# MLP up projections by seven half-token products for two tiles, with one low part of the weights on VectorE

## The chip, the cores and the metric

The program runs on one core of one Trainium2 chip. The metric is the device time of one launch in microseconds, as the median of several runs. TensorE (PE) multiplies and writes PSUM; VectorE (DVE), ScalarE (ACT) and GpSimd (POOL) do elementwise work; SyncE (SP) issues the loads of weights.

## The reference

Three transformer blocks over 512 tokens of width 1024. Two of them end in an MLP with a squared ReLU, and the change touches these alone:

```python
def squared_relu_mlp(h, w1, w2):
    return jnp.square(jax.nn.relu(h @ w1)) @ w2
...
        h = rms_norm(x, g[2])
        x = x + rms_norm(squared_relu_mlp(h, mlp_w1[i], mlp_w2[i]), g[3])
```

`w1` is 1024 x 4096 and `w2` 4096 x 1024, in float32. Before and after the MLPs stand attention, a convolution block and a gated feed-forward layer, which stay as they are.

## The kernel before

Activations lie transposed: 128 features on the partitions, 512 tokens along the free axis, 8 such tiles for a width of 1024. Every float32 operand is split into a high part (rounded to the matmul's format) and a low part (the difference), and every product is made of three matmuls: high x high, high x low, low x high (`products`, L1834 to L1836).

**Weights** come in blocks of 8 slots of 128x128, one block for one tile of outputs. There is a ring of 4 blocks in each of `raw`, `wh` and `wl`. For block n, SP loads `raw` when the low part of block n - 4 has been made (`load_range`), ScalarE copies it into `wh` when TensorE is through with block n - 4 (`hi`), and GpSimd subtracts the two into `wl` (`lo_range`, L548). TensorE waits for `w_lo`.

**The MLP** of a layer goes in 2 chunks of 16 hidden tiles. The up phase of a chunk has 16 tiles of 8 x 3 matmuls with 512 columns; the down phase has 8 output tiles with 16 x 3 matmuls each, from two blocks of weights. The up tiles rotate through four PSUM banks. Their input is the residual, not yet divided by its root mean square, so VectorE multiplies a tile by the square of that factor, `r2` (L1211), then makes max(z, 0) times that product with one `scalar_tensor_tensor` into a PSUM bank, `squared(j)` (L1219). ScalarE copies it into `HH` as the high part (L999), and VectorE subtracts the two into `HL` (L1211). The input of VectorE's instructions here is thus in PSUM on one side at least. In a down phase VectorE copies each finished bank to `M`, or adds it in the second chunk.

Every engine works through its own queue in the order of the program, and waits stand in it as instructions: what stands behind a wait waits too. Nothing else sets the order. `tmp` and `sqb` are buffers of 2 x 512 elements in SBUF, `RB`, `HB` and `META_BANK` are PSUM banks. The norms at both ends of an MLP use `HB`, `META_BANK`, `sqb` and `tmp` too.

## Time and profile before

| what | before |
|---|---|
| median of 3 runs | 1766.42 us (1766.36 to 1768.12) |
| profiled execution: its span, from the first to the last instruction | 1764.2 us |
| what lies between that span and the median of the runs | 2.2 us |
| instructions | 22985 |

The profile is of one execution. It gives that execution's time as its span; the times of the runs also hold what lies before the first and after the last instruction. In a row of the timeline the first number is the start in us from the start of the span, the second the duration; "x2" joins two instructions. A matmul's recorded duration is longer than its share of the array, since matmuls overlap: read the distance of their starts.

### The profile page before, as it was taken

To read this page: it belongs to the slowest core of one execution; us is meant where nothing else is said; L and a number is where in the kernel's file an instruction comes from. 1 tells how busy PE (TensorE), PEld (TensorE's weight loads), DVE (VectorE), ACT (ScalarE), POOL (GpSimd) and SP (SyncE) were. 2 spreads that over 40 slices of the span, in tenths; PEclk is the share of its full clock that TensorE was granted. 3 is DMA by queue.
4 is the path that set the end of the run, shared out by engine and by line. 5 is a ranking of instruction groups with operands and counts; after the bars stand their busy time and mean duration, and the time that the engine had idled before them with its cause. 6 is when DMAs were issued, how large, how long until landed. Compare 5 with 4: busy or idle time off the path is not lost.

```text
span 1764.2 us, 22985 instructions
## 1 busy us (share of the span) xinstructions
PE 1737.4 (98%) x8243; PEld 1445.3 (82%) x8243; DVE 785.8 (45%) x1225; ACT 662.9 (38%) x1039; POOL 876.9 (50%) x473
## 2 busy tenths in 40 slices
PE   8999999999999999999999999999999999999999
PEld 6887888888888877878888888889878888888887
DVE  6558654301331479956430133137856344444200
ACT  6338543312322456554321232135357332222221
POOL 3457545444444469755544444445445544444442
PEclk9999999999999999999999999999999999999999
DMA  5531123223333213123333332322210233332332
GB/s 190 133 98 59 37 72 107 95 95 96 96 96 99 80 48 108 60 84 95 103 99 96 96 95 95 95 84 72 87 49 14 95 95 96 97 101 98 96 107 71
DMA packets 46073, 158.45 MB, mean 90 GB/s; under 512 B 5744, under 2 KB 6000, under 8 KB 46000
## 3 DMA queue, kind: packets, MB, share of 16 engines
q1 hardware_dynamic: 46000, 157.45, 28.5%
q8 instruction: 49, 0.80, 0.2%
q14 instruction: 24, 0.20, 0.0%
HBM read 153.10 MB, written 2.10 MB: 88 GB/s over the span
## 4 chain that ended last, share of the span: by engine, by line
PE 90%; DVE 5%; ACT 2%; issue 1%; POOL 1%; DMA 0%; SPq 0%; DVEq 0%; POOLq 0%; ACTq 0%
PE PS L1834 26%; PE PS L1835 26%; PE PS L1836 26%; PE PS L1903 2%; DVE PS L1219 1%; PE PS L1939 1%; PE PS L1934 1%; PE PS L1935 1%; PE PS L2095 1%; PE PS L1844 1%; PE PS L1876 0%; PE PS L1976 0%; DVE PS L1211 0%; PE PS L2118 0%; PE PS L2119 0%
## 5 line engine op out<-in xcount | busy, mean ns | idle before, releaser
L548 POOL TENSOR_TENSOR wl<-raw,wh 128x1024 fp32r<-128x1024 f32 x216 | 523.0, 2422 | 623.2 <-ACT wh L742 198.3
L1835 PE MATMUL PS<-XLR,wh 128*128 128x512 f32 x1216 | 474.2, 390 | 0.0
L1834 PE MATMUL PS<-XHR,wh 128*128 128x512 f32 x888 | 348.8, 393 | 6.3 <-POOL wl L618 5.8
L1836 PE MATMUL PS<-XHR,wl 128*128 128x512 f32 x888 | 346.4, 390 | 0.0
L1834 PE MATMUL PS<-HH,wh 128*128 128x512 f32 x688 | 267.6, 389 | 0.0
L1835 PE MATMUL PS<-HL,wh 128*128 128x512 f32 x688 | 267.6, 389 | 0.0
L1836 PE MATMUL PS<-HH,wl 128*128 128x512 f32 x688 | 267.6, 389 | 0.0
L1835 PEld LDWEIGHTS PS<-XLR,wh 128*128 128x128 f32 x1216 | 229.1, 188 | 47.0
L728 ACT ACTIVATE wh<-raw 128x1024 fp32r<-128x1024 f32 x123 | 128.9, 1056 | 242.2 <-PE PS L1836 197.6
L1834 PEld LDWEIGHTS PS<-XHR,wh 128*128 128x128 f32 x888 | 167.4, 188 | 42.0 <-POOL wl L618 6.2
L1836 PEld LDWEIGHTS PS<-XHR,wl 128*128 128x128 f32 x888 | 167.4, 188 | 35.4
L1211 DVE TENSOR_TENSOR tmp<-PS,r2m 128x512 f32<-128x512 f32 x116 | 79.9, 691 | 253.2 <-PE PS L1836 235.7
L742 ACT ACTIVATE wh<-raw 128x1024 fp32r<-128x1024 f32 x68 | 72.1, 1061 | 284.3 <-PE PS L1836 284.3
L539 POOL TENSOR_TENSOR wl<-raw,wh 128x1024 fp32r<-128x1024 f32 x45 | 108.5, 2420 | 126.9 <-ACT wh L728 126.8
L1834 PEld LDWEIGHTS PS<-HH,wh 128*128 128x128 f32 x688 | 129.1, 188 | 26.9
L1836 PEld LDWEIGHTS PS<-HH,wl 128*128 128x128 f32 x688 | 129.1, 188 | 26.9
L1835 PEld LDWEIGHTS PS<-HL,wh 128*128 128x128 f32 x688 | 129.1, 188 | 26.7
L1834 PE MATMUL PS<-XF,wh 128*128 128x512 f32 x328 | 127.9, 390 | 0.1
L1836 PE MATMUL PS<-XF,wl 128*128 128x512 f32 x328 | 127.6, 389 | 0.0
L997 ACT ACTIVATE wh<-raw 128x1024 fp32r<-128x1024 f32 x56 | 59.4, 1060 | 164.2 <-PE PS L1836 164.2
L1190 ACT ACTIVATE wh<-raw 128x1024 fp32r<-128x1024 f32 x40 | 42.4, 1061 | 159.0 <-PE PS L1836 159.0
L578 POOL TENSOR_TENSOR prob<-prob,cols 128x512 f32<-128x512 f32 (+2 forms) x64 | 57.0, 893 | 40.8 <-DVE cols L1433 40.1
(344 smaller groups left out, 2561.6 us busy)
## 6 DMA issues: line engine op xcount, KB each, us to landing
raw<-weights SPq DMA_DIRECT2D x287, 512.0 KB, 3.5
X<-x_t SPq DMA_DIRECT2D x8, 256.0 KB, 6.7
out_t<-X SPq DMA_DIRECT2D x8, 256.0 KB, 4.7
KH<-rope_h SPq DMA_DIRECT2D x4, 128.0 KB, 4.7
KL<-rope_l SPq DMA_DIRECT2D x4, 128.0 KB, 5.5
QH<-XHR SPq DMA_DIRECT2D x16, 32.0 KB, 2.0
QL<-XLR SPq DMA_DIRECT2D x16, 32.0 KB, 2.0
pos_i<-positions SPq DMA_DIRECT2D x1, 256.0 KB, 8.5
```

What stands on the lines that cost most here:

```text
L539: pool.tensor_tensor(wl[:, n % RING], raw[:, n % RING], wh[:, n % RING].bitcast(F32), ALU.subtract).then_inc(w_lo, 1)
L548: pool.tensor_tensor(wl[:, j], raw[:, j], wh[:, j].bitcast(F32), ALU.subtract).then_inc(w_lo, 1)
L578: pool.tensor_tensor(p, p, cols[:, u % 4, 2:3].broadcast_to(p.shape), ALU.mult).then_inc(p_done, 1)
L728: sc.activation(wh[:, j], raw[:, j], ACT.Copy).then_inc(w_hi, 1)
L742: sc.activation(wh[:, j], raw[:, j], ACT.Copy).then_inc(w_hi, 1)
L997: sc.activation(wh[:, slot], raw[:, slot], ACT.Copy).then_inc(w_hi, 1)
L1190: sc.activation(wh[:, slot], raw[:, slot], ACT.Copy).then_inc(w_hi, 1)
L1211: return v.tensor_tensor(out, a, b, op)
L1834: pe.matmul(out, wa, xa, start=start, stop=False)
L1835: pe.matmul(out, wa, xb, start=False, stop=False)
L1836: return pe.matmul(out, wb, xa, start=False, stop=stop)
L1903: ins = pe.matmul(out[:, b], x, y[:, k, b * WIDE:(b + 1) * WIDE], start=first and k == 0, stop=last and k == KT - 1)
```

## The change

The hidden tiles of an MLP go in 4 chunks of 8, not 2 of 16. The up phase of the first chunk stays as it was, tile by tile. In the other three, two tiles make a group, which is computed as a product of matrices of two by two blocks: the two tiles, the two halves of the 1024 inputs (4 slots each), and the two halves of the tokens (256 columns each). Seven products of half blocks take the place of eight, in Winograd's form. Sums and differences of the four half blocks of weights of a group are made for each group; those of the four quarters of the activations once in a layer.

- **Activations.** During the down phase of the first chunk VectorE multiplies the residual by gain and factor into `CF` (`norm_halves`, eight instructions of 512), makes four combinations of 1024 (`combine_halves`), ScalarE makes seven high parts `CH`, and VectorE seven low parts `CL` in place of `CF`.
- **Weights of a group.** VectorE makes three sums of 512 into `sums` and in place in `raw` (`first_sums`) and a fourth later (`last_sum`), ScalarE five high parts (a11, s12 of double size, mid of double size, s4, a22). GpSimd makes the low parts of a11, s12, mid and s4; VectorE that of a22, the fourth raw half block (`low_a22`). The weights of the next group are made during the products of a group; those of the first group of a chunk during the down phase ahead of it.
- **Outputs of a group.** The products gather in two PSUM banks, `alpha` and `beta`, and a third, `gamma`. ScalarE copies what stands in them at four moments to the quarters of `tmp` (`z_part`), VectorE adds the other bank to three of them and squares each hidden tile in place, ScalarE copies it to `MH`, VectorE subtracts into `ML`. One buffer of 512 in `tmp` serves for each of the two tiles of a group.
- **Around it.** The down phases have 8 slots a tile and wait for each hidden tile by itself; VectorE copies to `M` in the first chunk and adds in three. A block "even" with one slot is put before the second MLP, so that its blocks start at an even slot of the ring. The loops of the MLP are unrolled. `low_taps` moves from the end of the first chunk's up phase to the last down phase of the first layer.

```diff
-CHUNK = 16
+CHUNK = 8
...
+HALF_K, HALF_T = KT // 2, S // 2
+PAIRS_UP = CHUNK // 2
+ORDER = [(i % 2) * PAIRS_UP + i // 2 for i in range(CHUNK)]
+COMBO = {name: i for i, name in enumerate(["b11", "t3", "b21", "b22", "t1", "t2", "t4"])}
+QUICK_GROUPS = PAIRS_UP * (NCHUNK - 1)
...
+        MH = at("MH", A, 0, [P, CHUNK, S], F32R)
+        ML = at("ML", A, 16 * KB, [P, CHUNK, S], F32R)
+        CH = at("CH", A, 32 * KB, [P, 7, HALF_K, HALF_T], F32R)
+        CL = at("CL", A, 60 * KB, [P, 7, HALF_K, HALF_T], F32R)
+        CF = at("CF", A, 60 * KB, [P, 7, HALF_K, HALF_T])
+        raw_halves = raw[:].rearrange("p r (h k) m -> p (r h) k m", h=2)
+        wh_halves = wh[:].rearrange("p r (h k) m -> p (r h) k m", h=2)
+        wl_halves = wl[:].rearrange("p r (h k) m -> p (r h) k m", h=2)
+        sums = sqb[:].rearrange("p h (k m) -> p h k m", m=P)
```

On SP, in the loop over groups of `load_groups`:

```diff
+                    for g in range(PAIRS_UP):
+                        n, q = n0 + 2 * g, up_group(layer, c, g)
+                        if g < 2:
+                            sp.wait_ge(w_lo, n - RING + 2)
+                        else:
+                            sp.wait_ge(a22_lo, q - 1)
+                        sp.dma_start(raw[:, (n + 1) % RING], weights[n + 1]).then_inc(raw_in[(n + 1) % RING], 16)
+                        if g >= 2:
+                            sp.wait_ge(w_lo, n - RING + 2)
+                        sp.dma_start(raw[:, n % RING], weights[n]).then_inc(raw_in[n % RING], 16)
```

On GpSimd, one of four alike and the order in a chunk:

```diff
+            def low_s12(n0, q):
+                h = slot_half(n0, 2)
+                pool.wait_ge(s12_hi, q + 1)
+                pool.tensor_tensor(wl_halves[:, h:h + 2], sums[:], wh_halves[:, h:h + 2].bitcast(F32),
+                                   ALU.subtract).then_inc(s12_lo, 1)
...
+                    low_a11(n0, n0, q0)
+                    low_s12(n0, q0)
+                    low_mid(n0, n0, q0)
+                    for g in range(PAIRS_UP):
+                        n, q = n0 + 2 * g, q0 + g
+                        if g < PAIRS_UP - 1:
+                            low_a11(n0, n + 2, q + 1)
+                        low_s4(n0, n)
+                        if g < PAIRS_UP - 1:
+                            low_s12(n0, q + 1)
+                            low_mid(n0, n + 2, q + 1)
```

On ScalarE, in the loop over groups of `quick_up`; `high_a11`, `high_s12` and `high_mid` wait for products 1, 3 and 5 of the group before, `high_a22` and `high_s4` for its last:

```diff
+                    high_a22(n0, n)
+                    sc.wait_ge(quick, 6 * q + 1)
+                    sc.wait_ge(hid, h0 + max(2 * g - 1, 0))
+                    sc.activation(z_part(0, 0), alpha(T0, g), ACT.Copy).then_inc(z_copied, 1)
+                    if g:
+                        sc.wait_ge(bank_free, T0 + 2 * g)
+                        sc.activation(MH[:, PAIRS_UP + g - 1], tmp[:, 1], ACT.Copy).then_inc(hid_hi, 1)
+                    if more:
+                        high_a11(n0, n + 2, q + 1, False)
+                    high_s4(n0, n, q)
+                    if not more:
+                        next_high(n + 2, 6 * q + 1)
+                    sc.wait_ge(quick, 6 * q + 2)
+                    sc.wait_ge(hid, h0 + 2 * g)
+                    sc.activation(z_part(1, 1), beta(T0, g), ACT.Copy).then_inc(z_copied, 1)
+                    sc.wait_ge(quick, 6 * q + 3)
+                    sc.activation(z_part(0, 1), alpha(T0, g), ACT.Copy).then_inc(z_copied, 1)
+                    if more:
+                        high_s12(n0, n + 2, q + 1, False)
+                        high_mid(n0, n + 2, q + 1, False)
+                    else:
+                        next_high(n + 3, 6 * q + 3)
+                        next_high(n + 4, 6 * q + 5)
+                    sc.wait_ge(z_squared, q + 1)
+                    sc.activation(MH[:, g], tmp[:, 0], ACT.Copy).then_inc(hid_hi, 1)
+                    sc.wait_ge(blocks_done, n + 2)
+                    sc.activation(z_part(1, 0), alpha(T0, g), ACT.Copy).then_inc(z_copied, 1)
+                hi(n0 + CHUNK + 3)
```

On VectorE:

```diff
+            def first_sums(n, q):
+                b0, b1 = first_half(n), first_half(n) + 2
+                v.wait_ge(raw_in[(n + 1) % RING], 16 * ((n + 1) // RING + 1))
+                v.wait_ge(s12_lo, q)
+                sig(tt(sums[:, 0], raw_halves[:, b1], raw_halves[:, b1 + 1], ALU.add), w_sums, 4 * q + 1)
+                v.wait_ge(raw_in[n % RING], 16 * (n // RING + 1))
+                sig(tt(sums[:, 1], sums[:, 0], raw_halves[:, b0], ALU.subtract), w_sums, 4 * q + 2)
+                sig(tt(raw_halves[:, b1], raw_halves[:, b0], raw_halves[:, b1], ALU.subtract), w_sums, 4 * q + 3)
+            def last_sum(n, q):
+                b0 = first_half(n) + 1
+                v.wait_ge(mid_lo, q + 1)
+                sig(tt(raw_halves[:, b0], raw_halves[:, b0], sums[:, 1], ALU.subtract), w_sums, 4 * q + 4)
+            def low_a22(n0, n, q):
+                h = slot_half(n0, 7)
+                v.wait_ge(a22_hi, q + 1)
+                tt(wl_halves[:, h], raw_halves[:, first_half(n) + 3], f(wh_halves[:, h]), ALU.subtract).then_inc(a22_lo, 1)
...
+                def low_hidden(x, done):
+                    v.wait_ge(hid_hi, done)
+                    tt(ML[:, x], tmp[:, x // PAIRS_UP], f(MH[:, x]), ALU.subtract).then_inc(hid, 1)
+                def square_second(g, q):
+                    v.wait_ge(z_copied, 4 * q + 4)
+                    stt(tmp[:, 1], tmp[:, 1], 0.0, tmp[:, 1], ALU.max, ALU.mult).then_inc(bank_free, 2)
+                for g in range(PAIRS_UP):
+                    n, q = n0 + 2 * g, q0 + g
+                    if g:
+                        low_hidden(g - 1, h0 + 2 * g - 1)
+                        square_second(g - 1, q - 1)
+                    last_sum(n, q)
+                    low_a22(n0, n, q)
+                    if g:
+                        low_hidden(PAIRS_UP + g - 1, h0 + 2 * g)
+                    if g < PAIRS_UP - 1:
+                        first_sums(n + 2, q + 1)
+                    v.wait_ge(quick, 6 * q + 4)
+                    v.wait_ge(z_copied, 4 * q + 3)
+                    tt(z_part(0, 0), z_part(0, 0), gamma(g), ALU.add).then_inc(z_added, 1)
+                    v.wait_ge(quick, 6 * q + 5)
+                    tt(z_part(1, 1), z_part(1, 1), alpha(T0, g), ALU.add).then_inc(z_added, 1)
+                    v.wait_ge(quick, 6 * q + 6)
+                    sig(tt(z_part(0, 1), z_part(0, 1), beta(T0, g), ALU.add), z_added, 3 * q + 3)
+                    stt(tmp[:, 0], tmp[:, 0], 0.0, tmp[:, 0], ALU.max, ALU.mult).then_inc(z_squared, 1)
+                low_hidden(PAIRS_UP - 1, h0 + CHUNK - 1)
+                square_second(PAIRS_UP - 1, q)
+                low_hidden(CHUNK - 1, h0 + CHUNK)
```

On TensorE:

```diff
+            def half_products(out, h, combo, start):
+                i = COMBO[combo]
+                for k in range(HALF_K):
+                    pe.matmul(out, wh_halves[:, h, k], CH[:, i, k], start=start and k == 0, stop=False,
+                              skip_group_check=True)
+                    pe.matmul(out, wh_halves[:, h, k], CL[:, i, k], start=False, stop=False, skip_group_check=True)
+                    ins = pe.matmul(out, wl_halves[:, h, k], CH[:, i, k], start=False, stop=k == HALF_K - 1,
+                                    skip_group_check=True)
+                return ins
+            def quick_group(n0, T0, g, q):
+                n, a, b, c = n0 + 2 * g, alpha(T0, g), beta(T0, g), gamma(g)
+                pe.wait_ge(a11_lo, q + 1)
+                if g < 2:
+                    pe.wait_ge(bank_free, T0 - 2 + 2 * g)
+                else:
+                    pe.wait_ge(z_copied, 4 * (q - 1))
+                half_products(a, slot_half(n0, 0), "b11", True).then_inc(quick, 1)
+                pe.wait_ge(s12_lo, q + 1)
+                if g >= 2:
+                    pe.wait_ge(z_added, 3 * (q - 1))
+                half_products(b, slot_half(n0, 2), "t1", True).then_inc(quick, 1)
+                pe.wait_ge(z_copied, 4 * q + 1)
+                half_products(a, slot_half(n0, 3), "t2", False).then_inc(quick, 1)
+                pe.wait_ge(mid_lo, q + 1)
+                half_products(c, slot_half(n0, 4), "b21", True).then_inc(quick, 1)
+                pe.wait_ge(z_copied, 4 * q + 3)
+                half_products(a, slot_half(n0, 5), "t3", False).then_inc(quick, 1)
+                pe.wait_ge(w_lo, n + 2)
+                half_products(b, slot_half(n0, 6), "b22", False).then_inc(quick, 1)
+                pe.wait_ge(a22_lo, q + 1)
+                pe.wait_ge(z_added, 3 * q + 2)
+                half_products(a, slot_half(n0, 7), "t4", False).then_inc(blocks_done, 2)
```

## Rows read from the trace of the kernel before

**Rows 1.** the page: busy time, share of the span and instructions by engine; the granted clock
```profile
PE 1737.4 (98%) x8243; PEld 1445.3 (82%) x8243; DVE 785.8 (45%) x1225; ACT 662.9 (38%) x1039; POOL 876.9 (50%) x473
...
PEclk9999999999999999999999999999999999999999
```

**Rows 2.** windows view of 250 to 600 us: busy us (x instructions) of PE, PEld, DVE, ACT, POOL
```profile
250.00:600.00 350.00, 349.67 (x1549) 288.98 (x1547) 99.29 (x144) 103.44 (x135) 161.33 (x71) 1.00 0.30 95
```

**Rows 3.** waits of TensorE, 251 to 600 us: waited for, us in total, times, longest
```profile
PE PS L1834 <- DVE PS L1219: 0.3, 1, 0.3
```

**Rows 4.** timeline of VectorE, up tiles: start us, us, engine line op names shapes [idle before]
```profile
322.57 0.69 DVE L1211 TENSOR_TENSOR tmp<-PS,r2m 128x512 f32<-128x512 f32 x1 [2.44 <-PE PS L1836]
...
328.01 0.69 DVE L1211 TENSOR_TENSOR tmp<-PS,r2m 128x512 f32<-128x512 f32 x1 [2.44 <-PE PS L1836]
```

**Rows 5.** timeline of TensorE in attention, first and last of eight matmuls, one weight load
```profile
195.77 0.28 PE L2118 MATMUL PS<-PH,VV 128*128 128x256 f32 x1
...
195.89 0.19 PEld L2118 LDWEIGHTS PS<-PH,VV 128*128 128x128 f32 x1
...
196.59 0.28 PE L2119 MATMUL PS<-PL,VV 128*128 128x256 f32 x1
```

**Rows 6.** chain that ended last: start us, us, what
```profile
1235.39 10.11 PE PS L1903 x84
```

**Rows 7.** groups by shape: busy us, mean ns | idle before
```profile
L599 POOL TENSOR_TENSOR XLR<-y_conv,XHR 128x512 fp32r<-128x512 f32 x4 | 5.0, 1286 | 0.1
...
L951 ACT ACTIVATE P2H<-PS 128x256 fp32r<-128x256 f32 x8 | 2.9, 357 | 0.0
...
L1211 DVE TENSOR_TENSOR wl<-raw,wh 128x1024 fp32r<-128x1024 f32 x4 | 4.9, 1225 | 1.9 <-ACT wh L728 1.8
...
L1211 DVE TENSOR_TENSOR P2L<-PS,P2H 128x256 fp32r<-128x256 f32 x8 | 3.2, 402 | 0.0
```

**Rows 8.** timeline of GpSimd and VectorE, both inputs in SBUF
```profile
1446.70 2.39 POOL L548 TENSOR_TENSOR wl<-raw,wh 128x1024 fp32r<-128x1024 f32 x1 [3.05 <-ACT wh L1190]
1447.17 2.46 DVE L1211 TENSOR_TENSOR tmp<-tmp,sqb 128x512 f32<-128x512 f32 x1 [0.92 <-ACT sqb L1178]
```

**Rows 9.** timeline of GpSimd and VectorE, one input in PSUM
```profile
301.95 2.40 POOL L548 TENSOR_TENSOR wl<-raw,wh 128x1024 fp32r<-128x1024 f32 x1 [3.04 <-ACT wh L997]
...
303.12 0.69 DVE L1211 TENSOR_TENSOR HL<-PS,HH 128x512 f32 x1 [0.88 <-ACT HH L999]
```

**Rows 10.** timeline of VectorE and GpSimd, VectorE first
```profile
557.28 0.69 DVE L1211 TENSOR_TENSOR tmp<-M 128x512 f32<-128x512 f32 x1
...
557.69 2.54 POOL L548 TENSOR_TENSOR wl<-raw,wh 128x1024 fp32r<-128x1024 f32 x1 [3.11 <-ACT wh L742]
```

**Rows 11.** timeline of both with work queued, and two of GpSimd in a row
```profile
1234.36 1.47 POOL L692 TENSOR_TENSOR pool_l<-pooled,pool_h 128x512 fp32r<-128x512 f32 x1
...
1235.32 1.07 DVE L1211 TENSOR_TENSOR pool_a<-u 128x527 f32<-128x527 f32 x1
...
1235.78 2.85 POOL L539 TENSOR_TENSOR wl<-raw,wh 128x1024 fp32r<-128x1024 f32 x1
...
1257.40 4.73 POOL L539 TENSOR_TENSOR wl<-raw,wh 128x1024 fp32r<-128x1024 f32 x2 [2.54 <-ACT wh L728]
```

**Rows 12.** timeline, handovers of an up tile, and a matmul that had waited
```profile
198.89 0.38 PE L2118 MATMUL PS<-PH,VV 128*128 128x256 f32 x1 [0.35 <-DVE PL L1211]
...
300.61 0.39 PE L1834 MATMUL PS<-XHR,wh 128*128 128x512 f32 x1
...
300.81 1.06 ACT L997 ACTIVATE wh<-raw 128x1024 fp32r<-128x1024 f32 x1 [3.28 <-PE PS L1836]
...
301.54 0.70 DVE L1219 SCALAR_TENSOR_TENSOR PS<-PS,tmp 128x512 f32<-128x512 f32 x1
...
302.37 0.60 ACT L999 ACTIVATE HH<-PS 128x512 f32 x1 [0.50 <-DVE PS L1219]
```

**Rows 13.** DMA issues of the page: KB each, median us from issue to landing
```profile
raw<-weights SPq DMA_DIRECT2D x287, 512.0 KB, 3.5
```

More of the change, by code:

```diff
@@ L1008, in _ @@
+                if layer == 0:
+                    sc.wait_ge(blocks_done, n0)
+                    sc.wait_ge(dw_low_done, 1)
+                    low_taps(0)
+                    low_taps(1)
+                hi_range(n0 + CHUNK, n0 + CHUNK + 3)
+                last_square(n0 + CHUNK)
             sc.wait_ge(vec_in, 32)
@@ L1062, in _ @@
                 sc.activation(XH[:, k], squared(k), ACT.Copy).then_inc(xh, 1)
-            hi_range(BLOCK0["pw2"] + 4, BLOCK0["pw2"] + 8 + 3)
+            hi_range(BLOCK0["pw2"] + 4, BLOCK0["even"])
+            hi(BLOCK0["even"])
+            for i in range(2):
+                hi(BLOCK0["mlp1_up0"] + i)
             sc.activation(exp_first[:], vec[:, 0:1], ACT.Sqrt)
@@ L1501, in _, with norm_halves @@
             outputs("w_out", "m1")
+            def norm_halves(layer, entry):
+                r = PS[:, RB].rearrange("p (h t) -> p h t", h=2)
+                for k in range(KT):
+                    first = COMBO["b21"] if k >= HALF_K else COMBO["b11"]
+                    stt(CF[:, first:first + 2, k % HALF_K], X[:, k].rearrange("p (h t) -> p h t", h=2),
+                        ENTRY_GAIN[entry](k), r, ALU.mult, ALU.mult).then_inc(norm_x, 1)
+                v.wait_ge(norm_x, KT * (layer + 1))
@@ new lines, in combine_halves, with low_halves @@
+            def combine_halves(layer):
+                b11, t3, b21, b22, t1, t2, t4 = (CF[:, i] for i in range(7))
+                n = 4 * layer
+                sig(tt(t1, t3, b11, ALU.subtract), combined, n + 1)
+                sig(tt(t2, b22, t1, ALU.subtract), combined, n + 2)
+                sig(tt(t3, b22, t3, ALU.subtract), combined, n + 3)
+                sig(tt(t4, b21, t2, ALU.subtract), combined, n + 4)
+            def low_halves(layer, parts):
+                for i in parts:
+                    v.wait_ge(combo_hi, 7 * layer + i + 1)
+                    tt(CL[:, i], CF[:, i], f(CH[:, i]), ALU.subtract).then_inc(combo_lo, 1)
@@ L1877, in spread, with tile @@
                 ins.then_inc(rb_done, 1)
-            def tile(n, T, hooks={}, high=XH, bank=None, order=range(KT), begun=False, ring=4):
+            def tile(n, T, hooks={}, high=XH, bank=None, order=range(KT), begun=False, ring=4, count=1):
                 if not begun:
@@ L2241, in _ @@
             for m in range(4, KT):
-                tile(BLOCK0["pw2"] + m, TILE0["pw2"] + m, bank=PS[:, RB] if m == KT - 1 else None)
+                tile(BLOCK0["pw2"] + m, TILE0["pw2"] + m, bank=PS[:, RB] if m == KT - 1 else None,
+                     count=2 if m == KT - 1 else 1)
             norm_out("m3", "mlp1_up0")
@@ L2428, in _pack_weights @@
             for i in range(CHUNK):
-                put(BLOCK0[f"mlp{layer}_up{c}"] + i, 0, up[c * CHUNK + i])
+                put(BLOCK0[f"mlp{layer}_up{c}"] + i, 0, up[c * CHUNK + ORDER[i]])
             for m in range(KT):
-                for b in range(2):
-                    k = c * CHUNK + b * SLOTS
-                    put(BLOCK0[f"mlp{layer}_down{c}"] + 2 * m + b, 0, down[m, k:k + SLOTS])
+                put(BLOCK0[f"mlp{layer}_down{c}"] + m, 0, down[m, c * CHUNK:(c + 1) * CHUNK])
     up = _tiles(odd_w_pw1[0], KT, 2 * KT)
```

240 lines of the change are left out of this document (184 added, 56 removed).

## The prediction

> **What bounds the kernel now.** I read the page's summary first: TensorE is busy 98% of a span of 1764.2 us, at a granted clock in the top tenth throughout (2.4 GHz), while GpSimd shows 50%, VectorE 45%, ScalarE 38% [rows 1]. The windows view of the first MLP, 250 to 600 us, has TensorE busy 349.67 of 350.00 us [rows 2], and the view of waits for that stretch holds one wait of a matmul, 0.3 us [rows 3]. So a matmul removed here is time removed, and a wait of TensorE added here is time added; the other engines have slack. An up tile of 24 matmuls (8 weight slots, three products) takes 5.44 us: VectorE starts the eviction of one tile at 322.57 and of the next at 328.01 [rows 4]. That is 226.7 ns for 512 columns, 10.88 us for a pair of tiles, 43.52 us for a chunk of eight.
>
> **What the change removes and adds on TensorE.** Three of four chunks of eight up tiles, in both layers, go by groups of two tiles: 12 groups a layer, 24 in all, 6 chunks. A group has 7 products of 4 slots and three matmuls, 84 matmuls of 256 columns, for 48 of 512. Eight matmuls with 256 columns in attention start from 195.77 to 196.59: 117 ns each, with a weight load ahead of each [rows 5]; 84 matmuls with 264 columns take 10.11 us, 120 ns each [rows 6]. I take 117.5 ns; bounds 113.3 (half of 226.7) and 120.4. A group is then 84 x 0.1175 = 9.87 us, 1.01 less than the pair; 24 groups save 24.2 us (bounds 32.7 and 18.4). The load alone is recorded with 190 ns [rows 5], but the starts show that it overlaps. The Trainium skill (TensorE: Matmul & The Clock Gate, section Back-to-back issue gap) gives N/2.4 + 2.5 ns, which at 256 columns is 109 ns; by that page a group would be 9.2 us and the saving some 41 us. Row and page differ, and no other term uses it.
>
> **What it adds elsewhere, for one inner group.** GpSimd takes 2.40 us for 1024 elements and two in a row 4.73, so a step of 2.37 [rows 9, 11]; 512 take 1.29 [rows 7], by the same difference a step of 1.25. ScalarE takes 1.06 for 1024 and 0.60 for 512 [rows 12], 0.36 for 256; VectorE 0.69 for 512 [rows 10], 0.40 for 256 with a PSUM input and 1.23 for 1024 [rows 7]. GpSimd makes four low parts: 1.25 + 2.37 + 2.37 + 1.25 = 7.2 us. VectorE makes 3 first sums, the last sum, the low part of the fourth half block, two squares and two low parts of hidden tiles, nine instructions of 512, and three additions of 256: 9 x 0.73 + 3 x 0.43 = 7.9. ScalarE makes 3 x 0.60 + 2 x 1.06 + 4 x 0.36 + 2 x 0.60 = 6.6. Each fits in 9.87 us on its own.
>
> They do not fit together. All nine of VectorE's instructions of 512 have both inputs in SBUF, and so have all of GpSimd's. Such an instruction of VectorE issued at 1447.17, while GpSimd ran from 1446.70 to 1449.09, took 2.46 us and not 0.69: it ended 0.54 after GpSimd's end [rows 8]. With one input in PSUM it takes 0.69 in the middle of GpSimd's work [rows 9]; this is how the present MLP does all of its up eviction, with the square in PSUM. The other way round, GpSimd issued 0.41 us into such an instruction, which takes 0.69, needs 2.54 and not 2.40 [rows 10]. Where both have work queued they alternate: VectorE ends at 1236.39, 0.56 after GpSimd's end, and GpSimd's next takes 2.85 [rows 11]. So the two exclude each other, and one of VectorE's costs the shared path some 0.55 us. An inner group needs 7.2 + 9 x 0.55 = 12.2 us of it: more than the 9.87 of TensorE and than the 10.88 of the pair before. (The low part moved from GpSimd to VectorE costs 0.55 there for 1.25.) The Trainium skill (SBUF — State Buffer, section SBUF: two separate sides) says that whoever starts first holds the shared port pair for the whole instruction and the other fully blocks; the trace agrees, but for the 0.15 us by which the start of the blocked one is hidden.
>
> **The walk.** I put the queues of one inner group in order, with these durations and the handovers of [rows 4, 9, 12]: 0.13 from VectorE to ScalarE, 0.15 back, 0.08 to GpSimd, 0.20 from a last matmul's successor to an evictor; a restart of TensorE costs 0.10 (0.38 for 0.28 in [rows 12]). Time 0 is the start of product 1. The two first sums of the next group end at -3.18; the two high copies of 1024 follow, ending at -1.99 and -0.93. GpSimd's low part of the first runs from -1.91 to 0.46. VectorE's first square is issued at -1.10, is held to 0.46 and ends at 1.01, not -0.40. GpSimd's next low part runs 0.88 to 3.25. ScalarE copies the hidden tile (to 1.74), the last quarter (2.10) and a high half block (2.70). The low part of the hidden tile, issued at 1.89, is held to 3.25 and ends at 3.80. Only then may ScalarE empty product 1 into that buffer, 3.93 to 4.29, for which product 3 waits: it starts at 4.35, product 2 ended at 2.82. **Stall 1.53.** Behind it on VectorE stand the second square, the last sum and the fourth half block's low part (5.99); the second hidden tile's low part is held by a GpSimd instruction that ends at 7.19 and ends at 7.74; ScalarE's two copies follow to 8.59, product 5 starts at 8.65, product 4 ended at 7.27. **Stall 1.38.** Product 7 waits 0.24 for an addition. With three restarts the group takes 9.87 + 3.45 = 13.32 us.
>
> The same walk at the edges: the first group of a chunk has its weights ready and no hidden tile behind it, 0; the second 0.75 + 1.38 + 0.24 + 0.30 = 2.67; the fourth, with no next group, 1.53 + 0.56 + 0.20 = 2.29. A chunk is 4 x 9.87 + 2.67 + 3.45 + 2.29 = 47.89. Behind it the first down tile needs the last hidden tile: its low part stands behind a square that is held by two whole-block low parts of GpSimd in turn, and the last three matmuls come 3.43 + 0.10 late. So a chunk costs 47.89 + 3.53 - 43.52 = 7.90 more, six chunks **47.4 us**.
>
> **Edits costed at nothing.** The normalised halves and their combinations (8 x 0.70, 4 x 1.23 and 7 x 1.23 us on VectorE, 7 x 1.06 on ScalarE, [rows 7, 12]) lie in the first down phase of each layer, 8 x 5.44 us long; without that cover they would add up to 26.5 us a layer. Extra additions into M stand where copies stood, at 0.69. The two weight loads of a group (1 MB in 9.87 us) start when the slots of two groups before come free and land in 3.5 us [rows 13]; SP waits in order there for VectorE's low part and GpSimd's, a group ahead of need. The dummy block costs one short transfer and one short instruction each on ScalarE and GpSimd, under pw2's matmuls. The code that is now unrolled I cost at nothing: the down phases of the stretch in [rows 2] are unrolled already, and it loses 0.33 us in all.
>
> **Sum.** 1764.2 + 47.4 = 1811.6 us for the span; the median of the runs lies 2.2 above the profiled span, hence 1813.8.
>
> **Rivals.** (a) TensorE keeps the pace, faster. If the holds fall where VectorE has room, only the 24.2 us count: 1766.4 - 24.2 = 1742. For it: each engine's own sum is below 9.87, and without holds the same walk has no stall at all. Against: the first stall needs only that a square is issued within GpSimd's two low parts of 1024, which start from the same product's end. It decides if the holds on the path sum to less than 1.0 us a group; I count 3.45. Chance 0.12. (b) The holds are harder: a held instruction pays its full 0.70, or GpSimd keeps its turn when it has work queued. The same walk gives 69 and 71 us: 1835 to 1837. For it: the skill's page as written; against: [rows 8, 11]. Chance 0.08. (c) The holds cost, but the order settles better than in my walk, gaining or losing under 30 us: 1745 to 1785. Chance 0.10, of which 0.02 within 3.5 us of before and 0.02 below. (d) The matmuls of 256 columns are bound by weight loads at 188 ns: 84 x 0.188 = 15.8 us, 1885; [rows 5] speaks against it, chance under 0.01. That the products are not cut does not arise: the loops state 84.
>
> **Chances and range.** Forecast 0.70. Faster by over 0.2% (which is about what a measurement here can tell) is (a) and the part of (c): 0.14; within it 0.02; slower 0.84. The range goes from 1776, where a third of my stalls would be gone, to 1838, the end of (b).
>
> **What would show it.** Right: SBUF-to-SBUF instructions of VectorE in the up chunks at 1.2 to 2.5 us, ending 0.55 behind GpSimd's; TensorE waiting for ScalarE's copies before products 3 and 5, some 13.3 us from group to group, and a wait of over 3 us in the first down tile; matmuls at 117 ns within a product. Wrong: groups 9.9 us apart, or TensorE waiting on weights, low parts of the raw block or DMAs instead.

## The result, and the profile after

The changed kernel takes 1814.4 us (median of 4 runs, 1811.5 to 1814.8) against 1766.4 us before: a ratio of 1.0266, 95% interval 1.0252 to 1.0281, 48 us slower. The prediction was 1813.8. The profiled execution has a span of 1812.5 us, 48.3 more than before.

The page after, its line of busy time, against [rows 1]:

```profile
PE 1741.2 (96%) x9107; PEld 1480.4 (82%) x9107; DVE 1031.5 (57%) x1435; ACT 744.1 (41%) x1222; POOL 968.4 (53%) x522
```

TensorE has 864 more matmuls and is busy 96%, not 98%. Waits of TensorE in the first MLP, 251 to 640 us (waited for, us in total, times, longest), against the one of [rows 3]; L2488 is a product of half blocks, L2163 a down tile, L696 GpSimd's low part for product 6:

```profile
PE PS L2163 <- DVE ML L1447: 9.5, 3, 3.2
...
PE PS L2488 <- ACT tmp L1178: 8.5, 9, 1.3
...
PE PS L2488 <- DVE tmp L1447: 2.7, 6, 0.5
...
PE PS L2488 <- POOL wl L696: 1.9, 6, 0.3
```

Per chunk (there are three a layer) that is one wait of 3.2 us in the first down tile, three before product 3, and two each of 0.3 and 0.5 us before products 6 and 7. The five other chunks of groups wait alike: over the whole run the totals are 18.9 us in 6 waits, 17.0 in 18, 3.9 and 5.5 in 12 each. They stand so in the timeline of TensorE, the first chunk of groups:

```profile
353.30 0.39 PE L2488 MATMUL PS<-CH,wh 128*128 128x256 f32 x1 [0.34 <-ACT tmp L1178]
...
358.20 0.39 PE L2488 MATMUL PS<-CH,wh 128*128 128x256 f32 x1 [0.33 <-POOL wl L696]
...
360.35 0.36 PE L2488 MATMUL PS<-CH,wh 128*128 128x256 f32 x1 [0.45 <-DVE tmp L1447]
...
366.15 0.39 PE L2488 MATMUL PS<-CH,wh 128*128 128x256 f32 x1 [1.25 <-ACT tmp L1178]
```

From product 3 at 353.30 to product 3 at 366.15 are 12.85 us, and as many to the next at 379.00: that is the group's length. Of the nine instructions of VectorE with both inputs in SBUF, a group like this one has four that are held. What VectorE and GpSimd do meanwhile, their rows from one timeline, in order of time (both inputs of each row are in SBUF):

```profile
348.44 2.39 POOL L690 TENSOR_TENSOR wl<-raw,wh 128x1024 fp32r<-128x1024 f32 x1 [0.27 <-ACT wh L1149]
...
349.13 2.25 DVE L1455 SCALAR_TENSOR_TENSOR tmp<-tmp 128x512 f32<-128x512 f32 x1
...
352.68 0.68 DVE L1455 SCALAR_TENSOR_TENSOR tmp<-tmp 128x512 f32<-128x512 f32 x1
...
353.29 0.68 DVE L1447 TENSOR_TENSOR raw<-raw,sqb 128x512 f32<-128x512 f32 x1
...
354.61 0.69 DVE L1447 TENSOR_TENSOR ML<-tmp,MH 128x512 fp32r<-128x512 f32 x1
354.63 1.82 POOL L678 TENSOR_TENSOR wl<-raw,wh 128x512 fp32r<-128x512 f32 x1 [3.80 <-ACT wh L1129]
...
355.22 1.78 DVE L1447 TENSOR_TENSOR sqb<-raw 128x512 f32<-128x512 f32 x1
...
356.41 1.74 POOL L696 TENSOR_TENSOR wl<-raw,wh 128x512 fp32r<-128x512 f32 x1
...
357.03 1.66 DVE L1447 TENSOR_TENSOR sqb<-sqb,raw 128x512 f32<-128x512 f32 x1
```

The square issued at 349.13 takes 2.25 us and ends at 351.38, 0.55 after GpSimd's end at 350.83, as in [rows 8]. From 354.6 the two take turns, as in [rows 11]: GpSimd's two low parts of 512 take 1.82 and 1.74 us for 1.29 [rows 7], VectorE's sums 1.78 and 1.66 for 0.69. The groups by shape, 251 to 625 us (busy us, mean ns), say it in sum:

```profile
L1455 DVE SCALAR_TENSOR_TENSOR tmp<-tmp 128x512 f32<-128x512 f32 x24 | 40.5, 1687 | 0.4
...
L1447 DVE TENSOR_TENSOR M<-M,PS 128x512 f32<-128x512 f32 x21 | 14.5, 688 | 79.1 <-PE PS L2165 79.1
```

The square, both inputs in SBUF, 1687 ns in the mean; the addition into M, one input in PSUM, 688.

What follows on the wait of 3.2 us stood in no term of the prediction. The timeline of TensorE in the first down tile:

```profile
390.92 0.40 PE L2165 MATMUL PS<-MH,wl 128*128 128x512 f32 x1
394.48 0.79 PE L2163 MATMUL PS<-MH,wh 128*128 128x512 f32 x1 [3.17 <-DVE ML L1447]
395.07 0.63 PE L2164 MATMUL PS<-ML,wh 128*128 128x512 f32 x1
395.50 0.63 PE L2165 MATMUL PS<-MH,wl 128*128 128x512 f32 x1
...
398.13 0.39 PE L2163 MATMUL PS<-MH,wh 128*128 128x512 f32 x1
```

The windows view of TensorE around it (us, PE busy (x instructions), PEclk, DMA share, GB/s):

```profile
386.00:391.00 5.00, 5.00 (x26) 1.00 0.64 224
...
394.40:398.00 3.60, 3.52 (x9) 0.54 0.24 90
398.00:403.00 5.00, 5.00 (x24) 1.00 0.00 0
```

Most matmuls behind the wait start 0.43 us apart, not 0.227, at a granted clock of 0.54, that is, most of this stretch at 1.2 and not 2.4 GHz. From 394.48 to 398.13 nine matmuls take 3.65 us for 9 x 0.227 = 2.04: 1.61 us lost, in which the restart itself, 0.1 us, is contained. Behind the waits of 1.25 us in the groups the granted clock stays at 1.00.

**The chunk's account.** From the first product at 339.84 to the first matmul of the down phase at 386.34 are 46.50 us, 2.98 more than the 43.52 of [rows 4]. The wait moves the last hidden tile's matmuls by 3.33 us (394.48 against 390.92 + 0.23), the slow restart behind it costs 1.61. The sum is 7.92 us, six chunks 47.5, of 48.3.

### The profile page after: what moved, and what is told of

It is laid out like the page before. It is cut to its first block, busy times and chain, and to the rows that moved or that the text cites. A ratio compares the mean times of both kernels' runs of the same rounds, so it can differ in the third digit from the quotient of the medians.

```text
span 1812.5 us, 24565 instructions
## 1 busy us (share of the span) xinstructions
PE 1741.2 (96%) x9107; PEld 1480.4 (82%) x9107; DVE 1031.5 (57%) x1435; ACT 744.1 (41%) x1222; POOL 968.4 (53%) x522
## 4 chain that ended last, share of the span: by engine, by line
PE 77%; DVE 15%; ACT 4%; issue 3%; POOL 1%; DMA 1%; SPq 0%; DVEq 0%; ACTq 0%; POOLq 0%
PE PS L2163 20%; PE PS L2165 20%; PE PS L2164 20%; DVE tmp L1455 4%; DVE sqb L1447 2%; PE PS L2232 2%; PE PS L2488 2%; DVE ML L1447 2%; PE PS L2491 2%; PE PS L2490 2%; DVE PS L1455 1%; DVE tmp L1447 1%; PE PS L2268 1%; PE PS L2263 1%; PE PS L2264 1%
## 5 line engine op out<-in xcount | busy, mean ns | idle before, releaser
L2164 PE MATMUL PS<-XLR,wh 128*128 128x512 f32 x832 | 324.6, 390 | 0.0
L865 ACT ACTIVATE wh<-raw 128x1024 fp32r<-128x1024 f32 x161 | 168.7, 1056 | 327.1 <-PE PS L2165 280.0
L2163 PE MATMUL PS<-MH,wh 128*128 128x512 f32 x512 | 203.3, 397 | 18.9 <-DVE ML L1447 18.9
L2488 PE MATMUL PS<-CH,wh 128*128 128x256 f32 x672 | 194.4, 289 | 26.4 <-ACT tmp L1178 17.0
L2163 PE MATMUL PS<-XHR,wh 128*128 128x512 f32 x504 | 199.1, 395 | 6.1 <-POOL wl L746 5.8
L2164 PE MATMUL PS<-ML,wh 128*128 128x512 f32 x512 | 202.5, 396 | 0.0
L2165 PE MATMUL PS<-MH,wl 128*128 128x512 f32 x512 | 202.3, 395 | 0.0
L2165 PE MATMUL PS<-XHR,wl 128*128 128x512 f32 x504 | 197.1, 391 | 0.0
L2490 PE MATMUL PS<-CL,wh 128*128 128x256 f32 x672 | 190.1, 283 | 0.0
L2491 PE MATMUL PS<-CH,wl 128*128 128x256 f32 x672 | 189.9, 283 | 0.0
L2488 PEld LDWEIGHTS PS<-CH,wh 128*128 128x128 f32 x672 | 128.5, 191 | 34.8 <-ACT tmp L1178 20.7
L2163 PEld LDWEIGHTS PS<-MH,wh 128*128 128x128 f32 x512 | 98.0, 191 | 42.5 <-DVE ML L1447 21.5
L2163 PE MATMUL PS<-XF,wh 128*128 128x512 f32 x328 | 127.9, 390 | 0.1
L2163 PEld LDWEIGHTS PS<-XHR,wh 128*128 128x128 f32 x504 | 95.2, 189 | 26.6 <-POOL wl L746 6.2
```

The costliest lines, as they stand in the source:

```text
L865: sc.activation(wh[:, j], raw[:, j], ACT.Copy).then_inc(w_hi, 1)
L2163: pe.matmul(out, wa, xa, start=start, stop=False)
L2164: pe.matmul(out, wa, xb, start=False, stop=False)
L2165: return pe.matmul(out, wb, xa, start=False, stop=stop)
L2488: pe.matmul(out, wh_halves[:, h, k], CH[:, i, k], start=start and k == 0, stop=False, skip_group_check=True)
L2490: pe.matmul(out, wh_halves[:, h, k], CL[:, i, k], start=False, stop=False, skip_group_check=True)
```

## The experiments

Nine kernels ran, each timed against the kernel before on the same chip; the intervals are of the ratio to it. "The walk" in the expectations is the queue-by-queue working of the prediction, done again with the durations and hand-overs read in the trace after. In this order: is it the port, is it the part that was moved, is it the clock, and then what order and port are worth each.

**e1.** In each of GpSimd's four low parts of a group:

```diff
+            def blank(out, s, n):
+                blanks[0] += 1
+                pool.memset(out.bitcast(F32), 0.0).then_inc(blanked, 1)
+                pool.wait_ge(blanked, blanks[0])
+                pool.memset(out.bitcast(F32), 0.0).then_inc(s, n)
...
-                pool.tensor_tensor(wl_halves[:, h:h + 2], sums[:], wh_halves[:, h:h + 2].bitcast(F32),
-                                   ALU.subtract).then_inc(s12_lo, 1)
+                blank(wl_halves[:, h:h + 2], s12_lo, 1)
```

> The changed kernel, but GpSimd's four low parts of a group (first half, the two sums, the two middle halves, fourth product's half) are each replaced by two memsets of the same low tiles, one waiting for the other: the low part of those weights is left out (zero). Same semaphores, same order, GpSimd as busy as before or nearly so, but it reads nothing from SBUF. Theory (VectorE's instructions with two SBUF inputs are held while GpSimd reads two tiles, and so what TensorE waits for is late): VectorE's sums, squares and hidden low parts fall from 1.2 to 2.9 us to about 0.7 us, the waits before products 3, 6 and 7 go, and of the wait in the first down tile some 2.4 us stay; walked through the queues that is 3.2 us a layer less than the kernel before, 1760 us, and up to 11 us more if TensorE's clock still falls after that wait: 1757 to 1777 us. Rival 1 (the waits come from the order of the queues and the hand-overs between engines, the port has little to do with it): 1805 to 1815 us. Rival 2 (GpSimd holds VectorE with writes as well): VectorE's rows stay at over 1.2 us and the time at about 1814.

Measured: 1768.2 us, ratio 0.9998 (0.9989 to 1.0008). VectorE's groups by shape, 251 to 625 us:

```profile
L1460 DVE SCALAR_TENSOR_TENSOR tmp<-tmp 128x512 f32<-128x512 f32 x24 | 22.9, 953 | 0.4
...
L1452 DVE TENSOR_TENSOR raw<-raw 128x512 f32<-128x512 f32 x12 | 8.3, 693 | 0.4
```

The 953 ns of the squares is a mean of two kinds: those within the groups take 0.69 us, those at the end of a chunk, beside whole-block low parts that still read SBUF, up to 2.78.

The one kind of wait of over 0.2 us that TensorE's matmuls have left in this stretch, 251 to 640 us:

```profile
PE PS L2168 <- DVE ML L1452: 6.8, 3, 2.8
```

The timeline of VectorE and of GpSimd, sums beside memsets, and then what stands for one low part of 1024:

```profile
362.83 0.53 POOL L682 MEMSET wl<- 128x512 f32 x1
362.85 0.68 DVE L1452 TENSOR_TENSOR sqb<-raw 128x512 f32<-128x512 f32 x1
...
363.57 0.69 DVE L1452 TENSOR_TENSOR sqb<-sqb,raw 128x512 f32<-128x512 f32 x1
363.94 0.52 POOL L682 MEMSET wl<- 128x512 f32 x1
...
365.42 0.96 POOL L680 MEMSET wl<- 128x1024 f32 x1 [0.95 <-ACT wh L1144]
366.43 0.95 POOL L682 MEMSET wl<- 128x1024 f32 x1
```

The sums take some 0.69 us while GpSimd writes. What is left is the last hidden tile's wait, behind whole-block low parts that e1 leaves as they are, with the clock's loss behind it: after the first chunk's wait of 1.99 us matmuls start 0.42 us apart, and the granted clock from 384 to 388 us is 0.81. So the waits in the groups need GpSimd's reading: with the same order and the same hand-overs, and without it, there are none. That the order has a part in them too, e6 shows. One reserve: two memsets of 1024 take 1.96 us for the low part's 2.40, so GpSimd is somewhat less busy too; that does not shorten an instruction of VectorE. The Trainium skill (SBUF — State Buffer, section SBUF: two separate sides) has an instruction of VectorE with two SBUF inputs exclude only an operation of GpSimd that reads SBUF; by that rule memsets cost VectorE nothing, and the trace agrees, with 693 ns.

**e2.** The low part of the fourth half block back on GpSimd:

```diff
@@ GpSimd, quick_lows
                         low_s4(n0, n)
+                        pool_a22(n0, n, q)
@@ VectorE, quick_up
-                    low_a22(n0, n, q)
```

> The changed kernel with the low part of the pair's fourth half block back on GpSimd, behind the low part for product 6, so that only the seven-product scheme is left of the change. Theory (the two engines share the way to SBUF, so that a low part costs the shared way its own length plus the 0.55 us hand-over whichever engine makes it, and GpSimd takes 1.25 us where VectorE takes 0.7): slightly slower than the changed kernel, 2.6 us a layer by the walk, 1819 us (1814 to 1826). Rival (VectorE is the late engine, GpSimd only 53% busy, so that giving the half back takes one of VectorE's nine held instructions of a group away and shortens its queue): 1800 to 1808 us.

Measured: 1825.2 us, ratio 1.0317 (1.0300 to 1.0334), at the upper end of the theory's range. The wait before product 7 has grown from 0.5 to 1.4 us, and TensorE waits for both last hidden tiles, 6 in place of 3, in the view of waits, 251 to 640 us:

```profile
PE PS L2169 <- DVE ML L1454: 11.4, 6, 3.2
...
PE PS L2494 <- DVE tmp L1454: 8.7, 6, 1.4
```

The part of the change that gives VectorE this low part is worth about 9 us (1.0317 against 1.0266 of 1766; by the two intervals 5 to 13). GpSimd shows 53% busy in the change, and it still helps to take 512 elements from it. The loss against before comes from the seven-product scheme.

**e3.** Spare matmuls in the wait:

```diff
                             if m == 0:
+                                if c and i == CHUNK - 1:
+                                    keep_busy(14, PS[:, HB])
                                 pe.wait_ge(hid, h0 + i + 1)
```

> The changed kernel with 14 spare 512-column matmuls into a bank that nobody reads (some 3.2 us at 227 ns) ahead of TensorE's wait for the last hidden tile in the first down tile of chunks 1 to 3. Nothing of the computation changes. Theory (the 3.2 us wait lowers the granted clock, and 8 to 9 matmuls behind it take 0.43 us in place of 0.227, some 1.8 us a chunk and 11 us for six chunks): the wait's length stays lost, the matmuls behind it take 0.227, and the time is 1803 us (1801 to 1807). Rival (the long matmuls are something else, for example the arrival of the weights or a bank shared with VectorE, which the filler doesn't touch): 1813 to 1816 us, and the 0.43 us matmuls stay where they are.

Measured: 1808.1 us (1805.0 to 1809.8), ratio 1.0226 (1.0209 to 1.0243). TensorE's timeline:

```profile
391.78 3.38 PE L2173 MATMUL PS<-ident_r 128*128 128x512 f32 x14
395.15 0.50 PE L2163 MATMUL PS<-MH,wh 128*128 128x512 f32 x1
395.49 0.39 PE L2164 MATMUL PS<-ML,wh 128*128 128x512 f32 x1
...
397.33 0.39 PE L2163 MATMUL PS<-MH,wh 128*128 128x512 f32 x1
```

The time without useful matmuls is as long as before (391.78 to 395.15), the matmuls behind it start 0.23 us apart again, and the granted clock is 1.00 throughout: the long matmuls are the clock, which had fallen behind the idle time. The gain of 0.4%, some 7 us, is less than the 11 expected: the nine matmuls from 395.15 to 397.33 take 2.18 us for 3.65, which is 1.47 a chunk and 9 in all, so that of the 1.61 us 0.14 is the restart; the other 2 us are within the spread of the runs. The Trainium skill (TensorE: Matmul & The Clock Gate, section Part 1: The HAM clock gate (the "warmup" mystery)) says that an idle TensorE falls back to half clock and has to be busy for a while before it comes back; the trace agrees.

**e5.** Two neighbours on ScalarE swapped:

```diff
-                hi(n0 + CHUNK + 3)
                 sc.wait_ge(bank_free, T0 + CHUNK)
                 sc.activation(MH[:, CHUNK - 1], tmp[:, 1], ACT.Copy).then_inc(hid_hi, 1)
+                hi(n0 + CHUNK + 3)
```

> The changed kernel with two neighbours swapped on ScalarE at the end of a chunk: the high part of the last hidden tile goes ahead of the high part of the whole block that is behind it in the trace of after. Nothing of the computation changes. Theory (the 3.2 us wait in the first down tile is for the most part queueing on ScalarE: the last square is there some 2.2 us before ScalarE has waited for TensorE's last group and copied the block, and GpSimd's hold on VectorE is the rest): the wait falls from 3.2 to 1.0 to 1.4 us, 2.2 us in each of six chunks, 13 us, and some or all of the 10 us that the clock costs behind it comes back: 1790 to 1801 us, 1794 taken. Rival (GpSimd's hold on the last square and its low part sets the wait, so that the order on ScalarE moves nothing): 1810 to 1816 us.

Measured: 1793.0 us, ratio 1.0148 (1.0131 to 1.0165). The size was right, the reason was not. The end of a chunk in the trace after, GpSimd, VectorE and ScalarE:

```profile
382.12 10.37 POOL L632 TENSOR_TENSOR wl<-raw,wh 128x1024 fp32r<-128x1024 f32 x4
...
390.19 2.85 DVE L1455 SCALAR_TENSOR_TENSOR tmp<-tmp 128x512 f32<-128x512 f32 x1
...
393.08 0.63 ACT L1204 ACTIVATE MH<-tmp 128x512 fp32r<-128x512 f32 x1 [3.74 <-DVE tmp L1455]
```

The same of e5, with TensorE's wait:

```profile
381.00 7.57 POOL L632 TENSOR_TENSOR wl<-raw,wh 128x1024 fp32r<-128x1024 f32 x3
...
389.05 0.68 DVE L1455 SCALAR_TENSOR_TENSOR tmp<-tmp 128x512 f32<-128x512 f32 x1
...
391.17 0.50 PE L2163 MATMUL PS<-MH,wh 128*128 128x512 f32 x1 [0.97 <-DVE ML L1447]
```

ScalarE had nothing to queue on: in the trace after it is idle for 3.74 us until the square is done. The square itself is long, 2.85 us in place of 0.69, because the block whose high part ScalarE made early gives GpSimd a fourth low part in a row, and the square is held by that one. With the swap GpSimd runs out of work after three, at 388.57, and the square is free. So it is the port again, reached through ScalarE's order. Behind this wait of 0.97 us the granted clock stays at 1.00. 2.2 + 1.6 us in six chunks are 23 us; 21 came.

**e6.** e5, and the order of three more steps (MH high part into the next group, `high_s4` ahead of `high_a11`, the second square ahead of the first low hidden part):

```diff
@@ ScalarE
                     high_a22(n0, n)
+                    if g:
+                        high_first(g - 1, q - 1)
...
+                    high_s4(n0, n, q)
                     if more:
                         high_a11(n0, n + 2, q + 1, False)
-                    high_s4(n0, n, q)
@@ VectorE
+                        square_second(g - 1, q - 1)
                         low_hidden(g - 1, h0 + 2 * g - 1)
-                        square_second(g - 1, q - 1)
```

> The changed kernel with the order of the queues alone changed, all tiles where they are: the swap of e5; ScalarE makes the first hidden high part of a group in the next group, behind the fourth half's high part, and the fourth product's high part ahead of the next first half's; VectorE squares the second tile ahead of the first low hidden part. Theory (port and order both cost: nine of VectorE's instructions of a group are held in any order, but fewer of them in front of what TensorE waits for): by the walk the wait before product 7 goes, those before product 3 (1.4 us) and product 6 (0.5 us) stay, 0.3 us is left in the first down tile, 5.6 us a layer above the kernel before: 1778 us (1772 to 1788). Rival 1 (order alone is the cause, rival c of the prediction): 1745 to 1765 us. Rival 2 (port alone, any order is as bad): 1790 us or more beyond what e5 gives.

Measured: 1777.7 us, ratio 1.0068 (1.0049 to 1.0088). TensorE's waits, 251 to 640 us:

```profile
PE PS L2494 <- ACT tmp L1185: 8.6, 9, 1.3
...
PE PS L2494 <- POOL wl L696: 2.0, 6, 0.3
```

Those before product 7 and in the first down tile are gone, those before products 3 and 6 stand. The low parts of the hidden tiles are not held in this order: 684 ns in the mean (251 to 625 us), against 1221 in the change. That all nine are held in any order, as the expectation has it, is thus not so. Of the 48 us, 35 were a matter of order (1.0266 against 1.0068), 21 of them by e5's swap; but in neither order tried with the tiles as they are does the scheme beat the kernel before.

**e4.** The squares into PSUM, order as in the change:

```diff
+        def square(f):
+            return PS[:, (STAT, META_BANK)[f]]
...
-                tt(ML[:, x], tmp[:, x // PAIRS_UP], f(MH[:, x]), ALU.subtract).then_inc(hid, 1)
+                tt(ML[:, x], square(x // PAIRS_UP), f(MH[:, x]), ALU.subtract).then_inc(hid, 1)
...
-                stt(tmp[:, 1], tmp[:, 1], 0.0, tmp[:, 1], ALU.max, ALU.mult).then_inc(bank_free, 2)
+                v.wait_ge(hid, h0 + max(2 * g, 0))
+                stt(square(1), tmp[:, 1], 0.0, tmp[:, 1], ALU.max, ALU.mult).then_inc(bank_free, 2)
```

> The changed kernel with one thing moved: VectorE writes the two squares of a group into two PSUM banks in place of over the sums in SBUF, ScalarE's high parts and VectorE's low parts of the hidden tiles are made from there (so that two of the nine instructions of VectorE in a group with both inputs in SBUF have only one there), ScalarE's copies of the next group's first and second partial sums wait for the squares and not for the hidden low parts, and the third accumulators all use one bank. All of the computation stays. Theory (port): the two low parts are no longer held, both squares still are; walked, the last hidden tile is 0.3 us late in place of 3.2, so that the clock's loss goes too, and the time is 4.2 us a layer above the kernel before, 1775 us (1769 to 1787). Rival (an instruction is held with one input in SBUF as well, or the waits come from hand-overs): 1800 us or more, with the low parts still at 1.2 us or more.

Measured: 1773.8 us, ratio 1.0036 (1.0022 to 1.0050). Groups by shape, 251 to 625 us:

```profile
L1461 DVE SCALAR_TENSOR_TENSOR PS<-tmp 128x512 f32<-128x512 f32 x24 | 40.8, 1700 | 0.4
L1453 DVE TENSOR_TENSOR ML<-PS,MH 128x512 fp32r<-128x512 f32 x32 | 22.1, 689 | 16.3 <-ACT MH L1205 8.0 <-ACT MH L1222 6.3 <-ACT MH L1210 2.0
```

The low parts, one input now in PSUM, fall from 1221 to 689 ns. The squares, which still read SBUF twice and only write to PSUM, stay at 1700: it is the inputs that count. Of the sums, the first is shorter too (1146 ns in the mean for 1421), the others are not. The same edit lets ScalarE refill `tmp` sooner, so that what it gains is not the port's alone.

**e7.** e4, and max(z, 0) by ScalarE into the bank, so that the square has an input there:

```diff
+                    sc.activation(square(0), tmp[:, 0], ACT.Relu).then_inc(relued, 1)
...
-                    stt(square(0), tmp[:, 0], 0.0, tmp[:, 0], ALU.max, ALU.mult).then_inc(z_squared, 1)
+                    tt(square(0), square(0), tmp[:, 0], ALU.mult).then_inc(z_squared, 1)
```

> e4 and one step more: ScalarE writes max(z, 0) of both hidden tiles of a group into the two PSUM banks, and VectorE multiplies that by z there, so that the squares have one input in PSUM as well: four of nine instructions with both inputs in SBUF are gone from a group, for two more ScalarE activations of about 0.6 us. The order of the queues is that of the change. Theory (port): the squares fall from 1.7 to 0.7 us; the walk leaves waits of 0.3 before product 3, 0.6 before product 7 and 0.6 us in the first down tile, 1.5 us a layer less than the kernel before: 1763 us (1758 to 1769). Rival (ScalarE is late with two more activations, a table is loaded, or two more hand-overs cost what the hold gave back): 1772 us or more.

Measured: 1760.8 us, ratio 0.9967 (0.9954 to 0.9981), with the squares at 700 ns in the groups by shape (251 to 625 us; five others of the same form are in the mean). The view of waits, 251 to 640 us, has this left before product 7:

```profile
L1460 DVE TENSOR_TENSOR PS<-PS,tmp 128x512 f32<-128x512 f32 x29 | 20.3, 700 | 14.1 <-ACT PS L1207 10.5 <-ACT PS L1214 3.4
...
PE PS L2502 <- DVE tmp L1460: 2.5, 6, 0.5
```

**e8.** e7 with another order (ScalarE: both hidden high parts between the first two copies, the second copy early, e5's swap; VectorE: low hidden parts behind the first sum and behind the additions):

In words, VectorE's order in a group:

```
e7: low_hidden 1, square 2, last_sum, low_a22, low_hidden 2, sums 1 to 3, additions 1 to 3, square 1
e8: square 2, last_sum, low_a22, sum 1, low_hidden 1, sums 2 and 3, additions 1 to 3, low_hidden 2, square 1
```

> e7 with the order of the queues changed: ScalarE makes both hidden high parts of a group in the next group, between its first and its second partial copy, and at the end of a chunk ahead of the next whole block's high part; the second copy goes ahead of the next first half's and the fourth product's high parts; VectorE puts the first low hidden part behind the first sum and the second one behind the group's three additions. Theory: with the hold taken off four of nine instructions and the queues ordered by what TensorE waits for, the walk has no wait left in the groups or in the first down tile, and what is left of the seven-product scheme is its whole saving, 10.6 us a layer by 0.119 us a matmul: 1745 us (1742 to 1754). Rival (the waits of 0.05 to 0.6 us that e7 leaves come from hand-overs that the walk prices too low, so that new ones take their place): 1755 to 1768 us.

Measured: 1748.7 us, ratio 0.9900 (0.9884 to 0.9917), within the range of the first theory. The page, busy time:

```profile
PE 1718.7 (99%) x9107; PEld 1470.9 (84%) x9107; DVE 951.7 (55%) x1435; ACT 771.2 (44%) x1270; POOL 951.6 (55%) x522
```

The windows view over most of the first chunk of groups and the start of its down phase (columns as in [rows 2]):

```profile
345.00:385.00 40.00, 40.00 (x311) 38.96 (x310) 26.55 (x40) 27.23 (x47) 32.11 (x16) 1.00 0.38 133
```

The timeline of TensorE, the chunk's first product and the first matmul of its down phase:

```profile
338.54 0.28 PE L2519 MATMUL PS<-CH,wh 128*128 128x256 f32 x1
...
378.90 0.40 PE L2194 MATMUL PS<-MH,wh 128*128 128x512 f32 x1
```

TensorE is busy without a gap. A chunk takes 40.36 us for 336 matmuls, 120.1 ns each, and saves 3.16 us: six save 19, and 1766.6 - 19 = 1747.6. This kernel beats both: 1.0% less than before, some 65 us less than the change.

**e9.** e8 with e2's edit.

> e8 with the low part of the pair's fourth half block back on GpSimd, behind the low part for product 6: the part of the change that moves this low part is undone, in a kernel in which TensorE no longer waits. Theory (the move is a real relief: it takes the shared way 0.55 to 0.7 us in place of 1.25 us and keeps GpSimd's queue short): the walk has waits of 0.1 to 0.35 us before products 6 and 7 of two groups of a chunk, 2.7 us a layer above e8: 1754 us (1750 to 1760). Rival (with TensorE's waits gone there is room in GpSimd's queue, 55% busy, and the move is worth nothing): 1747 to 1750 us.

Measured: 1758.1 us, ratio 0.9939 (0.9925 to 0.9952), 7 us above e8 by the ratios. TensorE has waits before product 6 again, most of them seen at the weight loads, in the view of waits, 251 to 640 us:

```profile
PEld PS L2525 <- POOL wl L701: 1.8, 4, 0.9
```

So the moved low part is worth 7 to 9 us with the waits and without.

## Why the prediction was right, and where it was not

**The bound and the side** were right: TensorE had no slack, every wait added is in the span. The scheme saves 19 us (e8), and waits and the clock cost some 67, three and a half times as much.

**The mechanism**, exclusion of the two engines where both of VectorE's inputs are in SBUF, is shown by three runs: e1 takes GpSimd's reads away and the groups' waits go; e4 gives the two low parts an input in PSUM, and they fall to 689 ns while the squares stay at 1700; e7 does it for the squares, and they fall to 700. Rival (a), that TensorE keeps pace at 1742, fell, though e8 shows what it described: 1748.7 once the holds are off the path. Rival (b), harder holds, fell: a held instruction ends 0.55 us behind GpSimd's, as predicted. Rival (c), the order settles better, fell as a forecast: the groups settle 1.4 us a chunk better than in the walk, but the time is far outside 1745 to 1785. Its bounds, besides, are some 20 us either way and not the "under 30 us" that it names. e6 shows that another order could have given 35 us. Rival (d), a bound by weight loads at 188 ns, has nothing for it: 120.

**The terms.** The matmul of 256 columns was taken at 117.5 ns and is 120.1 (e8), close to the upper bound: the saving is 19.0, not 24.2 us. The estimate of 109 ns by the Trainium skill (TensorE: Matmul & The Clock Gate, section Back-to-back issue gap) is not met; the page gives that formula for a matmul without its weight load. The group is 12.85 us, not 13.32: 10.09 for the matmuls and 2.76, not 3.45, of waits and restarts. Counted as the walk counts, from where the next matmul would have started (some 0.16 us more than the idle time in brackets in the rows), the stall before product 3 was there but a little smaller (1.41 for 1.53), that before product 5 (1.38) was not, and 0.48 before product 6 and 0.61 before product 7 (for 0.24) were; the restarts, 0.1 each, are as taken. The step that failed is the spacing of VectorE's instructions. The walk had them 0.73 us apart; that holds behind a sum, whose end the queue waits for (353.29, 354.00), but elsewhere they start 0.61 apart (352.68, 353.29) though they last 0.68. ScalarE's high parts follow each other closer too, 0.52 us apart for 0.60. So the second hidden tile's low part, which the walk has held by GpSimd to 7.74, slips in by 0.02 us (354.61, GpSimd at 354.63), and the two sums behind it were held instead; what they make late is product 6, for which GpSimd's turn comes after theirs, and the additions. The groups of a chunk came to 46.50 us, not 47.89.

**The end of the chunk**: a wait of 3.33 us, where 3.43 stood, for nearly the reason given: whole-block low parts in turn, of which one held the low part ahead of the square and the next the square. The clock's loss behind it, 1.47 us a chunk, is missing from the prediction. It makes good what the groups had too much: 4.37 + 3.53 = 7.90 predicted, 2.98 + 3.33 + 1.61 = 7.92 measured. That the total agrees to within 1 us is luck: groups and chunk's end are each off by 1.4 us a chunk, some 8 us in the sum, with opposite signs.

**The range** from 1776 is said to start where a third of the stalls would be gone. The walk's stalls and restarts are 2.67 + 3.45 + 2.29 + 3.53 = 11.94 us a chunk, 72 in all; a third less gives 1790, and 1776 takes half. The forecast itself does not rest on this.

**Edits costed at nothing** cost nothing that can be seen: in e8 they are all there, and its time is that of before less the saving, to within the 3 us of its interval.

**The count of the shared way** (7.2 + 9 x 0.55 = 12.2 us for an inner group) comes out of the runs better than the walk does. The third group of the first chunk, from product 1 to product 1, takes 12.85 us in the change and 12.18 in e6; by the same count, an estimate, e9 needs 10.7 and takes 10.75, and e8 needs 10.0, less than TensorE's 10.09, and takes 10.12. Where the order is poorer the group is longer than the count: 11.69 for 11.1 in e4, 10.80 for 10.0 in e7. So by this count the tiles as they are could not have reached TensorE's 10.09 in an inner group in any order.

Not tried: the three sums and the last sum with an input in PSUM, which are the holds that e8 still has, off the path (its sums take up to 1.67 us in the trace).

## What to carry to other kernels

Before giving VectorE more work beside GpSimd, count those of its instructions that take two inputs from SBUF: one that meets a reading instruction of GpSimd ended some 0.55 us behind it here, and the sum of both engines on that shared way, not either's busy share, has to fit in TensorE's time. Let one input come from PSUM, even if ScalarE has to put it there (0.6 us of ScalarE in e7). Then order each queue by what TensorE waits for next, and look at which step of a third engine hands GpSimd its next long instruction. Look behind a long wait of TensorE for matmuls at half clock: they belong to its price.

## What was not expected of the hardware

- Behind a wait of TensorE of 3.17 us eight matmuls started some 0.43 us apart, and behind one of 1.99 us (e1) matmuls started 0.42 apart; behind waits of 1.25 and 0.97 us none did.
- VectorE's instructions of 0.68 us start 0.61 us apart when none of them waits; behind one whose end the queue waits for, it is 0.71.
- Matmuls of 256 columns, each with a weight load, run 120.1 ns apart over a chunk, where 512 columns take 226.7: half the columns cost 53% of the time.
